# Router logits computed tile by tile inside the mix projection, first gather indices written by VectorE, gate splits behind the router

## The chip, the cores and the metric

One core of one Trainium2 chip runs the whole kernel in one launch. The metric is device time in microseconds (us). All times below are of that core.

## The reference

Two transformer-like blocks run one after the other on 1024 tokens of width 1024. The change touches the seam between attention and the mixture of experts in the first block. Cut to that:

```python
h = h + mix @ w_out[l]                      # mix projection, 1024 x 1024
xn = rmsnorm(h, ffn_norm_g[l])
g_prob = softmax(xt @ wg + bg)              # 4 groups
g_top_p, g_top_i = lax.top_k(g_prob, 1)
e_logits = (xt @ we + be)                   # 32 experts, the 8 of the chosen group
top_val, top_idx = lax.top_k(e_logits, 2)
# tokens are sorted into blocks of 128 per expert: buf_tok, block_e
xb = x_pad[buf_tok]                         # gather
h1 = silu(xblk @ w_gate[e]) * (xblk @ w_up[e]); y = h1 @ w_down[e]
```

The 4 group logits and 32 expert logits of a token are one product with a 1024 x 36 matrix. After the router, the tokens of each expert are gathered and go through its three weight matrices.

## The kernel before

The kernel is written engine by engine, each with its own program, and semaphores join them. Matrix products are made of fp16 halves: every fp32 operand is split into a high part (ScalarE, `..._hi`) and a low part (VectorE, `..._lo`), and `product` issues three matmuls (L409, L410, L411) for high by high, high by low and low by high.

**Mix projection.** Tokens are cut in 8 tiles of 128 (`TT`). For tile t TensorE runs two groups of 24 matmuls of 512 columns (`group`, banks of the PSUM tensor `ps`). VectorE adds the result to the residual (L1499), ScalarE takes the norm's statistics (L441, L442), VectorE scales to `xn` (L454). Two iterations later TensorE transposes `xn` of the tile (`transposes(pe, 2, t - 2, ...)`, 8 matmuls, L463) into the PSUM tensor `pt`, ScalarE copies the high part (`xt_hi`, L469), VectorE the low part (`xt_lo`, L475). `pt` has four banks. A transposed tile takes two of them, and `tpair(t % 2)` alternates between banks 0, 1 and banks 2, 3, so that the transposes of a tile wait for the low part of the tile but one before. Two tiles of transposes are left when the last group is done.

**Logits.** After all tiles TensorE computes the router logits: 8 tiles x 8 slices x 3 matmuls of 36 columns into bank 0 of `ps`, then one increment of `s_lg`.

**Router.** `router` on VectorE is a chain of some 60 small instructions, each waiting for the one before. It goes to TensorE three times and back. It ends with a table of which token stands in which place of which expert block: 16 matmuls (L1898) give the column numbers, VectorE turns them to integers (`tok_of`, L845) and increments `s_slots`. Just before that copy stand four small instructions for blocks beyond the first 32 (L838 to L843).

**Experts.** For block e, `gather` on GpSimd copies one column of `tok_of` to a fixed place (`idx[q]`, L997) and issues an indirect DMA by it (L1000). `x_transposes` on TensorE (L1908), `xe_hi` on ScalarE (L1178) and `xe_lo` on VectorE (L1518) make the halves of the gathered tokens in banks 0, 1 of `pt`. TensorE's order is transposes of block 0, transposes of block 1 (which wait for the low part of block 0), gate product of block 0, up product of block 0, gate product of block 1, and so on. The weights stand in slots: up in 0 and 1, gate in 2 and 3, down in 4 and one unsplit. `expert_hi` (L542) and `expert_lo` (L546) split them. VectorE splits the gate slots of expert 0 ahead of the router, the up slots behind it. SyncE loads the next expert's weights into a slot as soon as both halves of the present ones are made.

```python
            for i in range(2):
                expert_lo(dve, 2 + i, 0)
            router(dve, ch)
            for i in range(2):
                expert_lo(dve, i, 0)
            for q in range(2):
                xe_lo(q, q)
```

Of the kernel before, what the change touches and what calls it, by code (L numbers as in the profile page):

```python
# [15 lines left out]
P = 128  # L16
# [90 lines left out]
def build(nc, a, out):  # L107
    with ExitStack() as ctx:
# [52 lines left out]
        idx = [cols[:, 144 + i:145 + i].bitcast(I32) for i in range(2)]  # L161
        over_e = cols[0:1, 146:146 + NOVER + 1].bitcast(I32)
# [293 lines left out]

        def transposes(pe, r, t, src):
            n = TT * r + t
            pe.wait_ge(s_xn, n + 1)
            if n >= 2:  # L460
                pe.wait_ge(s_xl, n - 1)
            for k in range(KT):
                i = nc.tensor.transpose(tpair(t % 2)[:, k, :], src(t, k), ident)  # L463
            i.then_inc(s_tr, 1)

        def xt_hi(act, r, t):
            act.wait_ge(s_tr, TT * r + t + 1)
            dst = xh2(t) if r == 4 else XH[:, :, t * P:(t + 1) * P]
            nc.scalar.activation(dst, tpair(t % 2), ACT.Copy).then_inc(s_xh, 1)  # L469

        def xt_lo(dve, r, t):
            dve.wait_ge(s_xh, TT * r + t + 1)
            hi = xh2(t) if r == 4 else XH[:, :, t * P:(t + 1) * P]
            lo = xl2(t) if r == 4 else XL[:, :, t * P:(t + 1) * P]
            nc.vector.tensor_tensor(lo, tpair(t % 2), hi, ALU.subtract).then_inc(s_xl, 1)  # L475
# [85 lines left out]
        def overflow(eng, body):  # L561


            eng.wait_ge(s_slots, 1)
            n = eng.value_load(n_over, min_val=0, max_val=NOVER)
            with eng.If(n > 0):
                with eng.Fori(0, NOVER) as j:
                    with eng.If(j < n):
                        body(j)
# [178 lines left out]
        def router(dve, ch):  # L748
# [4 lines left out]
            dve.wait_ge(s_lg, 1)  # L753
            ch.done(V_.scalar_tensor_tensor(
                out=rL, in0=PS[:, 0, 0:TT * 36].rearrange("p (t c) -> p t c", t=TT), scalar=IWS,
# [80 lines left out]
            i.then_inc(s_rt, 1)  # L836

# [5 lines left out]
            V_.tensor_copy(n_over, rinc[0:1, NE - 1:NE])  # L843
            dve.wait_ge(s_rp, 3)
            V_.tensor_copy(tok_of, PS[:, 0, 0:BLK_MAX + 1]).then_inc(s_slots, 1)  # L845
# [107 lines left out]
        def _(pool):  # L953
# [41 lines left out]
            def gather(e, q):  # L995

                nc.gpsimd.tensor_copy(idx[q], tok_of[:, bass.ds(e, 1)]).then_inc(s_ix, 1)  # L997
                pool.wait_ge(s_ix, e + 1)
# [342 lines left out]
        def _(dve):  # L1341
# [166 lines left out]
            for i in range(2):  # L1508
                expert_lo(dve, 2 + i, 0)
            router(dve, ch)  # L1510


            for i in range(2):
                expert_lo(dve, i, 0)
# [217 lines left out]
        def _(pe):  # L1732
# [126 lines left out]
            for t in range(2):  # L1859
                transposes(pe, 1, t, mixed)  # L1860
            for t in range(TT + 2):
                if t < TT:
                    pe.wait_ge(s_xl, TT + t + 1)
                    for c in range(2):
                        g = 48 + 2 * t + c
                        group(pe, g, (12 + 2 * c, 13 + 2 * c), False, 0, t)
                        if g < 51:
                            for u in range(2):
                                transposes(pe, 1, 2 * (g - 47) + u, mixed)
                if t >= 2:  # L1870
                    transposes(pe, 2, t - 2, from_xn)

            pe.wait_ge(s_rws, 1)
            pe.wait_ge(s_xl, 3 * TT)
            for b in range(4):
                pe.wait_ge(s_free[b], 16)
            for t in range(TT):
                for k in range(KT):
                    tk, c = slice(t * P, (t + 1) * P), slice(k * 36, k * 36 + 36)
                    i = product(pe, PS[:, 0, t * 36:(t + 1) * 36], XH[:, k, tk], XL[:, k, tk], rwh[:, c], rwl[:, c],  # L1880
                                k == 0, k == KT - 1)
            i.then_inc(s_lg, 1)
# [284 lines left out]
```

## Time and profile before

| | us |
|---|---|
| median of 3 runs | 2337.84 |
| lowest, highest | 2336.97, 2340.63 |
| the profiled execution | 2341.51 |
| its span in the trace | 2339.8 |
| TensorE matmul busy | 2128.6 (91%) |
| VectorE busy | 1234.3 (53%) |
| ScalarE busy | 906.5 (39%) |

A row of the chain of waits gives start, length and what ran, followed back from the last instruction. A row of the timeline gives start, length, engine, line, operation, output and inputs, and in brackets how long the engine stood idle and what ended that. PE is TensorE, PEld its weight loads, DVE is VectorE, ACT ScalarE, POOL GpSimd, SPq the DMA queue of SyncE. Times are from the span's start.

### The profile page before, as it was taken

Reading aid. Unit: us, or ns where it says so; the run is one execution under the profiler, and the core shown is the slowest. Engines: PE = TensorE matmul, PEld = TensorE weight load, DVE = VectorE, ACT = ScalarE, POOL = GpSimd, SP = SyncE. Lnnn points to the kernel's source line nnn. Section 1 sums busy time; section 2 is a strip of 40 time slices with the busy share of each in tenths; the row PEclk is TensorE's granted clock in tenths of the full one; section 3 lists DMA queues with packets and bytes.
Section 4 is the critical chain, followed back from the end, with each engine's and each line's share of the span. In section 5 each row is a group of like instructions: output and inputs, shape, how many; then the busy total and the mean of one; then the engine's idle time right before and its main releaser. Section 6 shows DMA issues by size and latency. Waiting matters only on the chain.

```text
span 2339.8 us, 28085 instructions
## 1 busy us (share of the span) xinstructions
PE 2128.6 (91%) x10811; PEld 1091.7 (47%) x10811; DVE 1234.3 (53%) x1374; ACT 906.5 (39%) x1219; POOL 199.1 (9%) x264
## 2 busy tenths in 40 slices
PE   5998988888399999999945899959999999999999
PEld 3445446644244445445423465544444444444444
DVE  4225237744688888888867152384534343343432
ACT  4122126722267666666744152372312112211210
POOL 1000031000111111111120010022000000000000
PEclk9999999999699999999977899979999999999999
DMA  9101220051399999999975043325201011010001
GB/s 380 56 37 37 63 54 1 1 210 55 111 416 422 422 412 417 417 413 417 408 266 225 28 153 113 98 85 180 73 36 72 36 56 52 36 72 36 36 0 72
DMA packets 77020, 378.62 MB, mean 162 GB/s; under 512 B 12368, under 2 KB 19152, under 8 KB 44368
## 3 DMA queue, kind: packets, MB, share of 16 engines
q1 hardware_dynamic: 54000, 296.82, 32.1%
q0 software_dynamic: 22944, 80.75, 9.7%
q8 instruction: 52, 0.85, 0.2%
q14 instruction: 24, 0.20, 0.0%
HBM read 326.67 MB, written 37.75 MB: 156 GB/s over the span
## 4 chain that ended last, share of the span: by engine, by line
PE 86%; DVE 7%; issue 3%; DMA 2%; ACT 1%; SPq 1%; POOL 1%; POOLq 0%; DVEq 0%; ACTq 0%
PE ps L409 22%; PE ps L411 22%; PE ps L410 22%; PE pt L1954 5%; PE pt L409 1%; PE pt L410 1%; PE pt L411 1%; PE pt L1908 1%; DVE cols L1441 1%; PE pt L463 1%; PE pt L1844 1%; PE pt L2010 1%; PE pt L2012 1%; PE pt L2011 1%; DMA resid<-in_x 1%
## 5 line engine op out<-in xcount | busy, mean ns | idle before, releaser
L409 PE MATMUL ps<-xt,split 128*128 128x512 f16 x960 | 370.3, 386 | 22.8 <-issue 13.8
L409 PE MATMUL ps<-split,xt 128*128 128x512 f16 x928 | 354.5, 382 | 25.5 <-DMA xt<-arena 20.0
L410 PE MATMUL ps<-xt,split 128*128 128x512 f16 x960 | 369.7, 385 | 0.0
L411 PE MATMUL ps<-xt,split 128*128 128x512 f16 x960 | 369.4, 385 | 0.0
L411 PE MATMUL ps<-split,xt 128*128 128x512 f16 x928 | 354.4, 382 | 0.0
L410 PE MATMUL ps<-split,xt 128*128 128x512 f16 x928 | 354.3, 382 | 0.0
L546 DVE SCALAR_TENSOR_TENSOR split<-stage,split 128x2048 f16<-128x2048 f32 x128 | 290.1, 2287 | 57.8 <-ACT split L542 57.8
L542 ACT ACTIVATE split<-stage 128x2048 f16<-128x2048 f32 x128 | 237.1, 1901 | 121.1 <-PE ps L411 121.1
L411 PE MATMUL ps<-split,arena 128*128 128x512 f16 x512 | 194.3, 379 | 0.0
L410 PE MATMUL ps<-split,arena 128*128 128x512 f16 x512 | 194.3, 379 | 0.0
L409 PE MATMUL ps<-split,arena 128*128 128x512 f16 x512 | 194.3, 379 | 0.0
L1723 DVE SCALAR_TENSOR_TENSOR resid<-ps,resid 128x512 f32<-128x512 f32 x128 | 87.2, 690 | 191.7 <-PE ps L411 191.6
L409 PEld LDWEIGHTS ps<-xt,split 128*128 128x128 f16 x960 | 95.0, 99 | 139.0 <-issue 27.0
L1708 DVE TENSOR_TENSOR arena<-arena 128x512 f32<-128x512 f32 x64 | 44.3, 692 | 218.6 <-ACT arena L1322 218.6
L669 ACT ACTIVATE split<-stage 128x2048 f16<-128x2048 f32 x32 | 59.4, 1900 | 252.9 <-PE ps L411 252.9
L409 PEld LDWEIGHTS ps<-split,xt 128*128 128x128 f16 x928 | 91.3, 98 | 135.8 <-issue 35.2
L411 PEld LDWEIGHTS ps<-xt,split 128*128 128x128 f16 x960 | 95.2, 99 | 117.2 <-issue 6.9
L410 PEld LDWEIGHTS ps<-xt,split 128*128 128x128 f16 x960 | 95.1, 99 | 114.7 <-issue 5.5
L410 PEld LDWEIGHTS ps<-split,xt 128*128 128x128 f16 x928 | 91.2, 98 | 112.5 <-issue 12.5
L411 PEld LDWEIGHTS ps<-split,xt 128*128 128x128 f16 x928 | 91.2, 98 | 111.0 <-issue 2.7
L1322 ACT ACTIVATE arena<-ps 128x512 f32<-128x512 f32 x64 | 38.2, 597 | 244.1 <-PE ps L411 244.1
L1954 PE MATMUL pt<-arena,xt 128*128 128x512 f32 x256 | 115.1, 593 | 0.0
(291 smaller groups left out, 3010.3 us busy)
## 6 DMA issues: line engine op xcount, KB each, us to landing
stage<-in_w_gate SPq DMA_DIRECT2D x64, 1024.0 KB, 7.9
stage<-in_w_up SPq DMA_DIRECT2D x64, 1024.0 KB, 8.0
arena<-in_w_down SPq DMA_DIRECT2D x64, 1024.0 KB, 9.9
stage<-in_w_mlp SPq DMA_DIRECT2D x32, 1024.0 KB, 5.3
y_rows<-arena POOLq DMA_DIRECT2D x48, 512.0 KB, 8.7
arena<-in_conv_taps POOLq DMA_DIRECT2D x32, 576.0 KB, 4.3
stage<-in_w_dense_a SPq DMA_DIRECT2D x16, 1024.0 KB, 8.9
stage<-in_w_dense_b SPq DMA_DIRECT2D x12, 1024.0 KB, 9.0
```

What stands on the lines that cost most here:

```text
L409: nc.tensor.matmul(out_ap, lh, rh, start=start, stop=False)
L410: nc.tensor.matmul(out_ap, lh, rl, start=False, stop=False)
L411: return nc.tensor.matmul(out_ap, ll, rh, start=False, stop=stop)
L463: i = nc.tensor.transpose(tpair(t % 2)[:, k, :], src(t, k), ident)
L542: nc.scalar.activation(whi(s), wstage(s), ACT.Copy, scale=WS).then_inc(s_wh[s], 1)
L546: nc.vector.scalar_tensor_tensor(out=wlo(s), in0=wstage(s), scalar=WS, in1=whi(s), op0=ALU.mult, op1=ALU.subtract).then_inc(s_wo[s], 1)
L669: nc.scalar.activation(whi(s), wstage(s), ACT.Copy, scale=WS).then_inc(s_wh[s], 1)
L1322: nc.scalar.activation(relu[j % 2], PS[:, j % 4, :], ACT.Relu, scale=IWS)\
L1441: nc.vector.tensor_reduce(negmax[:, 2 * b + m:2 * b + m + 1], SC(m)[:, 0:W], AX.X, ALU.max, negate=True).then_inc(s_amx, 1)
L1708: nc.vector.tensor_tensor(relu2[j % 2], relu[j % 2], relu[j % 2], ALU.mult).then_inc(s_relu, 1)
L1723: nc.vector.scalar_tensor_tensor(out=H[:, t, hs], in0=PS[:, j % 4, :], scalar=IWS, in1=H[:, t, hs], op0=ALU.mult, op1=ALU.add).then_inc(s_ ...
L1954: m = nc.tensor.matmul(PT[:, 3, :], hTf[:, k, :], native(q)[:, k * UC:k * UC + UC], start=k == 0, stop=k == UK - 1)
```

## The change

Three things are done.

1. The logits of a tile are computed by a new function `logits(t)`, into bank 2 of `pt`. Tiles 0 to 4 come inside the mix projection, between the two groups of tiles 3 to 7. Tiles 5, 6 and 7 come between and behind the last transposes. Since bank 2 is taken, the transposes of this stage (r = 2) all use banks 0 and 1 (`tpar`), and each waits for the low part of the tile just before. Each of the eight `logits` increments `s_lg`, and the router waits for 8.
2. VectorE writes two columns of integer tokens straight to `idx[0]` and `idx[1]`, then `tok_of`, both ahead of the four small instructions. GpSimd's first two gathers have no copy of their own. The overflow code waits for a second increment of `s_slots`.
3. VectorE splits the gate slots behind the router: `router`, then slots 2, 3, 0, 1.

```diff
+        def tpar(r, t):
+            return tpair(0 if r == 2 else t % 2)
         def transposes(pe, r, t, src):
             n = TT * r + t
             pe.wait_ge(s_xn, n + 1)
-            if n >= 2:
+            if r == 2:
+                pe.wait_ge(s_xl, n)
+            elif n >= 2:
                 pe.wait_ge(s_xl, n - 1)
...
-            dve.wait_ge(s_lg, 1)
+            dve.wait_ge(s_lg, TT)
...
             i.then_inc(s_rt, 1)
+            dve.wait_ge(s_rp, 3)
+            V_.tensor_copy(idx2, PS[:, 0, 0:2])
+            V_.tensor_copy(tok_of, PS[:, 0, 0:BLK_MAX + 1]).then_inc(s_slots, 1)
...
-            V_.tensor_copy(n_over, rinc[0:1, NE - 1:NE])
-            dve.wait_ge(s_rp, 3)
-            V_.tensor_copy(tok_of, PS[:, 0, 0:BLK_MAX + 1]).then_inc(s_slots, 1)
+            V_.tensor_copy(n_over, rinc[0:1, NE - 1:NE]).then_inc(s_slots, 1)
...
             def gather(e, q):
-                nc.gpsimd.tensor_copy(idx[q], tok_of[:, bass.ds(e, 1)]).then_inc(s_ix, 1)
-                pool.wait_ge(s_ix, e + 1)
+                if not (isinstance(e, int) and e < 2):
+                    nc.gpsimd.tensor_copy(idx[q], tok_of[:, bass.ds(e, 1)]).then_inc(s_ix, 1)
+                    pool.wait_ge(s_ix, e - 1)
...
-            for i in range(2):
-                expert_lo(dve, 2 + i, 0)
             router(dve, ch)
-            for i in range(2):
-                expert_lo(dve, i, 0)
+            for s in (2, 3, 0, 1):
+                expert_lo(dve, s, 0)
...
+            def logits(t):
+                pe.wait_ge(s_rws, 1)
+                pe.wait_ge(s_xl, 2 * TT + t + 1)
+                for k in range(KT):
+                    tk, c = slice(t * P, (t + 1) * P), slice(k * 36, k * 36 + 36)
+                    i = product(pe, PT[:, 2, t * 36:(t + 1) * 36], XH[:, k, tk], XL[:, k, tk], rwh[:, c], rwl[:, c],
+                                k == 0, k == KT - 1)
+                i.then_inc(s_lg, 1)
             for t in range(TT + 2):
                 if t < TT:
                     pe.wait_ge(s_xl, TT + t + 1)
...
+                        if c == 0 and t >= 3:
+                            logits(t - 3)
                 if t >= 2:
                     transposes(pe, 2, t - 2, from_xn)
+                if t >= TT:
+                    logits(t - 3)
+            logits(TT - 1)
```

On TensorE, at the end of the mix projection, stood before: the last matmuls, three tiles of transposes (5, 6, 7), then 192 matmuls of 36 columns (line numbers of the changed kernel are one to some ten higher).

```order
2154 L411 MATMUL ps<-split,xt 128x512
2155 L463 MATMUL pt<-misc,xn 128x128 [waits xt_lo,norm_xn]
2156 L463 MATMUL pt<-misc,xn 128x128 x7
2157 L463 MATMUL pt<-misc,xn 128x128 [waits xt_lo,norm_xn]
2158 L463 MATMUL pt<-misc,xn 128x128 x7
2159 L463 MATMUL pt<-misc,xn 128x128 [waits xt_lo,norm_xn]
2160 L463 MATMUL pt<-misc,xn 128x128 x7
2161 L409 MATMUL ps<-zone,xt 128x36 [waits bank_free1,bank_free2,bank_free0,bank_free3,xt_lo,router_split]
```

And at the same place now:

```order
2274 L412 MATMUL ps<-split,xt 128x512
2275 L470 MATMUL pt<-misc,xn 128x128 [waits xt_lo,norm_xn]
2276 L470 MATMUL pt<-misc,xn 128x128 x7
2277 L470 MATMUL pt<-misc,xn 128x128 [waits xt_lo,norm_xn]
2278 L470 MATMUL pt<-misc,xn 128x128 x7
2279 L410 MATMUL pt<-zone,xt 128x36 [waits xt_lo,router_split]
...
2302 L412 MATMUL pt<-zone,xt 128x36
2303 L470 MATMUL pt<-misc,xn 128x128 [waits xt_lo,norm_xn]
2304 L470 MATMUL pt<-misc,xn 128x128 x7
2305 L410 MATMUL pt<-zone,xt 128x36 [waits xt_lo,router_split]
```

24 of the small matmuls stand between the transposes of tiles 6 and 7, 48 behind them, and the other 120 have moved ahead of this place, 24 at a time.

On VectorE, from the end of the router to the first gathered block, stood before (`router_products` is `s_rp`, `w_hi` the high half of a weight slot, `x_hi` the high half of a gathered block):

```order
406 L834 TENSOR_TENSOR junk<-junk,misc 128x384
407 L838 TENSOR_TENSOR arena<-arena,misc 1x512
408 L841 TENSOR_REDUCE arena<-arena 1x16 [waits dve_step]
409 L842 TENSOR_SCALAR cols<-arena 1x16 [waits dve_step]
410 L843 CAST cols<-arena 1x1
411 L845 CAST cols<-ps 128x48 [waits router_products]
412 L546 SCALAR_TENSOR_TENSOR split<-stage,split 128x2048 [waits w_hi0]
413 L546 SCALAR_TENSOR_TENSOR split<-stage,split 128x2048 [waits w_hi1]
414 L1518 TENSOR_TENSOR xt<-pt,xt 128x1024 [waits x_hi] x2
```

And now:

```order
404 L841 TENSOR_TENSOR junk<-junk,misc 128x384
405 L845 CAST cols<-ps 128x2 [waits router_products]
406 L846 CAST cols<-ps 128x48
407 L848 TENSOR_TENSOR arena<-arena,misc 1x512
408 L851 TENSOR_REDUCE arena<-arena 1x16 [waits dve_step]
409 L852 TENSOR_SCALAR cols<-arena 1x16 [waits dve_step]
410 L853 CAST cols<-arena 1x1
411 L553 SCALAR_TENSOR_TENSOR split<-stage,split 128x2048 [waits w_hi2]
412 L553 SCALAR_TENSOR_TENSOR split<-stage,split 128x2048 [waits w_hi3]
413 L553 SCALAR_TENSOR_TENSOR split<-stage,split 128x2048 [waits w_hi0]
414 L553 SCALAR_TENSOR_TENSOR split<-stage,split 128x2048 [waits w_hi1]
415 L1523 TENSOR_TENSOR xt<-pt,xt 128x1024 [waits x_hi] x2
```

The integer copies moved ahead of the four small instructions, and four splits stand where two stood.

On GpSimd, behind the eight stores of `xn`, stood before:

```order
27 L997 COPY cols<-cols 128x1 [waits slots_known,norm_transposed,xn_stored1,xn_stored0]
28 L1000 DMA xt<-xn_rows,cols 128x1024 [waits index_column]
29 L997 COPY cols<-cols 128x1
30 L1000 DMA xt<-xn_rows,cols 128x1024 [waits index_column]
31 L997 COPY cols<-cols 128x1 [waits x_gathered0,x_transposed]
```

And now:

```order
27 L1009 DMA xt<-xn_rows,cols 128x1024 [waits norm_transposed,slots_known,xn_stored0,xn_stored1]
28 L1009 DMA xt<-xn_rows,cols 128x1024
29 L1006 COPY cols<-cols 128x1 [waits x_gathered0,x_transposed]
```

The two copies ahead of the first two indirect DMAs are gone.

## Rows read from the trace of the kernel before

**Rows 1.** The page, part 4: shares of the chain that ended last

```profile
PE 86%; DVE 7%; issue 3%; DMA 2%; ACT 1%; SPq 1%; POOL 1%; POOLq 0%; DVEq 0%; ACTq 0%
```

**Rows 2.** Chain of waits, 500 to 660 us: start, length, what ran

```profile
613.40 3.87 POOL cols L997
...
618.15 6.47 DMA xt<-xn_rows,cols
624.76 1.95 PE pt L1908 x8
...
627.79 1.24 DVE xt L1518
629.16 1.94 PE pt L1908 x8
631.11 0.43 PE ps L409
```

**Rows 3.** Timeline, VectorE, 570 to 665 us

```profile
577.54 1.23 DVE L475 TENSOR_TENSOR xt<-pt,xt 128x1024 f16<-128x1024 f32 x1 [1.06 <-ACT xt L469]
...
582.39 1.23 DVE L475 TENSOR_TENSOR xt<-pt,xt 128x1024 f16<-128x1024 f32 x1 [1.11 <-ACT xt L469]
584.19 4.49 DVE L546 SCALAR_TENSOR_TENSOR split<-stage,split 128x2048 f16<-128x2048 f32 x2 [0.57 <-ACT split L542]
589.46 0.46 DVE L754 SCALAR_TENSOR_TENSOR arena<-ps,zone 128x288 f32<-128x288 f32 x1 [0.78 <-PE ps L411]
...
611.06 0.67 DVE L838 TENSOR_TENSOR arena<-arena,misc 1x512 f32<-1x512 f32 x1
...
612.63 0.18 DVE L845 CAST cols<-ps 128x48 int32<-128x48 f32 x1
612.74 4.47 DVE L546 SCALAR_TENSOR_TENSOR split<-stage,split 128x2048 f16<-128x2048 f32 x2
```

**Rows 4.** Timeline, TensorE, 574 to 613 us

```profile
574.19 1.04 PE L463 MATMUL pt<-misc,xn 128*128 128x128 f32 x8
576.53 1.09 PE L463 MATMUL pt<-misc,xn 128*128 128x128 f32 x8 [1.30 <-DVE xn L454]
...
588.34 0.18 PE L411 MATMUL ps<-zone,xt 128*128 128x36 f16 x1
...
588.94 0.18 PE L411 MATMUL ps<-zone,xt 128*128 128x36 f16 x1
...
611.20 0.82 PE L1898 MATMUL ps<-junk,arena 128*128 128x48 f16 x16 [9.94 <-DVE junk L834]
```

**Rows 5.** Windows: stretch, length, busy time by engine, then clock, DMA share, GB/s

```profile
570.00:574.00 4.00, 4.00 (x21) 1.78 (x19) 0.00 (x0) 0.00 (x0) 0.00 (x0) 1.00 0.00 0
...
581.00:582.00 1.00, 0.30 (x3) 0.06 (x1) 0.29 (x1) 0.66 (x1) 0.00 (x0) 0.71 0.46 188
...
588.00:589.00 1.00, 1.00 (x45) 1.00 (x42) 0.69 (x1) 0.00 (x0) 0.00 (x0) 0.87 0.71 262
...
700.00:800.00 100.00, 100.00 (x451) 49.56 (x450) 85.03 (x58) 68.34 (x58) 16.11 (x18) 1.00 1.01 422
```

**Rows 6.** Timeline, ScalarE, 570 to 665 us

```profile
577.66 1.02 ACT L469 ACTIVATE xt<-pt 128x1024 f16<-128x1024 f32 x1 [0.16 <-PE pt L463]
```

**Rows 7.** Timeline, GpSimd and VectorE, where experts end and combining begins

```profile
1206.09 2.78 POOL L1045 DMA_INDIRECT arena<-y_rows,cols  x1 [4.13 <-issue]
...
1215.08 0.94 POOL L1045 DMA_INDIRECT arena<-y_rows,cols  x1 [0.30 <-issue]
...
1201.31 8.90 DVE L595 SCALAR_TENSOR_TENSOR split<-stage,split 128x2048 f16<-128x2048 f32 x4 [0.44 <-issue]
1215.07 2.61 DVE L1573 SCALAR_TENSOR_TENSOR resid<-arena,cols,resid 128x1024 f32<-128x1024 f32 x2 [4.86 <-DMA arena<-y_rows,cols]
```

**Rows 8.** Timeline, SyncE's DMA queue, 570 to 665 us

```profile
586.56 2.55 SPq L536 DMA_DIRECT2D stage<-in_w_gate  x2
615.10 2.93 SPq L536 DMA_DIRECT2D stage<-in_w_up  x2
```

More of the change, by code:

```diff
@@ L161, in build @@
         idx = [cols[:, 144 + i:145 + i].bitcast(I32) for i in range(2)]
+        idx2 = cols[:, 144:146].bitcast(I32)
         over_e = cols[0:1, 146:146 + NOVER + 1].bitcast(I32)
@@ L459, in transposes @@
             pe.wait_ge(s_xn, n + 1)
-            if n >= 2:
+            if r == 2:
+                pe.wait_ge(s_xl, n)
+            elif n >= 2:
                 pe.wait_ge(s_xl, n - 1)
             for k in range(KT):
-                i = nc.tensor.transpose(tpair(t % 2)[:, k, :], src(t, k), ident)
+                i = nc.tensor.transpose(tpar(r, t)[:, k, :], src(t, k), ident)
             i.then_inc(s_tr, 1)
@@ L468, in xt_hi @@
             dst = xh2(t) if r == 4 else XH[:, :, t * P:(t + 1) * P]
-            nc.scalar.activation(dst, tpair(t % 2), ACT.Copy).then_inc(s_xh, 1)
+            nc.scalar.activation(dst, tpar(r, t), ACT.Copy).then_inc(s_xh, 1)
         def xt_lo(dve, r, t):
@@ L474, in xt_lo @@
             lo = xl2(t) if r == 4 else XL[:, :, t * P:(t + 1) * P]
-            nc.vector.tensor_tensor(lo, tpair(t % 2), hi, ALU.subtract).then_inc(s_xl, 1)
+            nc.vector.tensor_tensor(lo, tpar(r, t), hi, ALU.subtract).then_inc(s_xl, 1)
         FM = [True, False, False, True, True, False]
@@ L561, in overflow @@
         def overflow(eng, body):
-            eng.wait_ge(s_slots, 1)
+            eng.wait_ge(s_slots, 2)
             n = eng.value_load(n_over, min_val=0, max_val=NOVER)
@@ L752, in router @@
             tok = misc[:, M_TOK:M_TOK + TT]
-            dve.wait_ge(s_lg, 1)
+            dve.wait_ge(s_lg, TT)
             ch.done(V_.scalar_tensor_tensor(
-                out=rL, in0=PS[:, 0, 0:TT * 36].rearrange("p (t c) -> p t c", t=TT), scalar=IWS,
+                out=rL, in0=PT[:, 2, 0:TT * 36].rearrange("p (t c) -> p t c", t=TT), scalar=IWS,
                 in1=rb.unsqueeze(1).to_broadcast([P, TT, 36]), op0=ALU.mult, op1=ALU.add))
@@ L1869, in _ @@
                                 transposes(pe, 1, 2 * (g - 47) + u, mixed)
+                        if c == 0 and t >= 3:
+                            logits(t - 3)
                 if t >= 2:
                     transposes(pe, 2, t - 2, from_xn)
-            pe.wait_ge(s_rws, 1)
-            pe.wait_ge(s_xl, 3 * TT)
+                if t >= TT:
+                    logits(t - 3)
+            logits(TT - 1)
             for b in range(4):
                 pe.wait_ge(s_free[b], 16)
[L1877 to L1882, printed above, removed]
             pe.wait_ge(s_rt, 1)
```

## Prediction

> **What bounds the kernel now.** I read the shares of the chain first: TensorE holds 86% of it [rows 1], so time is won where TensorE stands still or does work that could be elsewhere. The chain in order of time then shows the one long stretch where it does: from the last groups of the mix projection to the gate product of expert 0. TensorE waits there in turn for the router, for a 3.87 us copy on GpSimd, for a 6.47 us indirect DMA, and for the round through ScalarE and VectorE, until 631.11 [rows 2]. Behind it, in the expert loop, TensorE is busy in 100.00 of 100 us, and ahead of it, in the mix projection, in 4.00 of 4 us [rows 5]. So all that counts is the moment at which the gate product starts. What makes it earlier is won in full, and what is added to the mix projection is lost in full.
>
> I count from two moments: S = 574.19, when the transposes of tile 5 start [rows 4], and R = 589.46, when the router's first instruction starts [rows 3]. R is S + 15.27.
>
> **Logits inside the projection: +3.0.** The logits at the end ran mostly at the lower clock; the clock rose to 2.4 GHz at the end of the 588 to 589 window (granted 0.87 on average), and from there the rows stand 0.025 us apart: 24 of them take 588.94 - 588.34 = 0.60 us [rows 4, 5]. Inside the projection the clock is high, so a tile costs 0.60 us, and five tiles (0 to 4) cost 3.0 us on an engine that has no slack. Nothing hides this. The bounds are 2.0 (if 36 columns cost by their number) and 4.0 (if each switch between 512 and 36 columns costs 0.2 more). Their operands are ready: the low part of the tile is a whole group old. S moves by +3.0.
>
> **The tail: -2.0.** Before, the transposes of tile 6 started at 576.53, beside the low part of tile 5, since they used other banks. Now they wait for it: it ends at 577.54 + 1.23 = 578.77, which is S + 4.6 [rows 3, 4]. From a tile's transposes to ScalarE's copy pass 577.66 - 576.53 = 1.13, the copy takes 1.02 [rows 6], and the low part 1.23: 3.4 us with the hand-over. So tile 6 is done at S + 8.0, and only then may tile 7 be transposed. At full clock it is done at S + 11.5. Before, the clock fell in the 581 to 582 window (0.71), 6 us after the dense work of the projection ended, though two tiles of transposes lay between [rows 5]. Now tile 7's transposes come 7 us after it. I take them at 1.2 GHz: 1.95 for eight instead of 1.09 [rows 2, 4], so S + 12.3. The logits of tiles 5 and 6 lie beside the waits. Those of tile 7 take 24 x 0.03 and a drain of 0.2, 0.9 us, so the router starts at S + 13.2 instead of S + 15.27: -2.0 (at full clock -3.0). The 7 x 0.7 us of logits that go from here are so half eaten by the single pair of banks. With the +3.0 before S, the router starts 1.0 us later than now.
>
> **Gate splits behind the router.** Ahead of the router they cost nothing: 584.19 to 588.68, beside the logits [rows 3]. With logits short they would now hold the router up, so moving them is what makes the shorter tail worth anything. Behind the router there is no cover but the gather.
>
> **From router to gate product: -5.0.** The router itself does not change. Its last matmuls end at 611.20 + 0.82 = 612.02 [rows 4]. VectorE now copies at once: 612.1 to 612.35 with 0.18 each, overlapping as consecutive ones do; before, the copy ended at 612.81, behind the four small instructions. These follow, from 611.06 to 612.74 before, less the copy: 1.6 us, so the splits start at 613.9. Four take 8.90 [rows 7]: 622.8. Then comes the low part of block 0 with 1.24, to 624.0; the transposes of block 1 0.14 later, as before (629.16 after 627.79 + 1.24), with 1.95: the gate product starts at 626.1 against 631.11, if the gather is ready [rows 2, 3].
>
> The gather: 0.6 us passed from the copy's end to GpSimd's (612.81 to 613.40) and 0.9 from that one's end to the DMA (617.27 to 618.15) [rows 2, 3]. One wait is left, so the DMA starts between 613.0 and 613.9, lands 6.47 later, by 619.5 to 620.4, and the low part may start 627.79 - 624.76 = 3.03 after that, at 622.5 to 623.4. VectorE is free at 622.8. The two ways to the low part are level: I add 0.2. So the 4.8 us that the GpSimd copy and its hop give back are real, but VectorE's two added splits stand right behind them. Any further speed of the gather would be worth nothing.
>
> **Loads.** A slot is reloaded when both its halves are made. The gate loads of expert 1 went out at 586.56, the up loads at 615.10 [rows 8]. They now go out from 616 to 623, four of 1 MB, beside the gathers. At the loop's 422 GB/s [rows 5] 4 MB and the two gathers take 12 us, so all is there by about 629; ScalarE first needs them when the gate product is over, some 6 us after 626.1. Free, if the gathers are not held up by them; if they are, by up to 1.4 us.
>
> **Sum.** +3.0 - 2.0 - 5.0 + 0.2 = -3.8 us. The profiled execution took 2341.51, 1.7 more than its span and 3.7 more than the median; the terms are differences, so 2341.51 becomes 2337.7 and the median 2337.84 becomes 2334.0.
>
> **Rival 1, full clock in the tail (2333.1).** If the clock has not yet fallen at S + 8, the last round is 0.85 shorter and the last logits 0.1: -4.75. For it: the drop came only 6 us after the dense work. Against: by then there have been two long waits of TensorE.
>
> **Rival 2, the port (2339.1, or 2343.3 at worst): slower.** The GpSimd copy that took 3.87 ended at 617.27, and the two splits beside it at 612.74 + 4.47 = 617.21 [rows 2, 3]. It seems to have waited for them. If an indirect DMA is held off by splits in the same way, it now meets four of them. The second gather is issued near 614.7, within the splits in any case. Held to 622.8 it lands at 629.3, and the gate product starts at 631.2, 5.1 later than summed: 2334.0 + 5.1 = 2339.1. The first gather is issued at 613.0 to 613.9, the splits start at 613.9; if it misses that moment too, it lands at 629.3, the low part starts at 632.3, the gate product at 635.6: +9.5 - 0.2, so 2343.3, slower than before. For it: an indirect DMA issued at 1206.09 inside four splits took 2.78 instead of 0.94. Against: it ended at 1208.87, 1.3 before those splits did (1210.21), so it got in between two of them; and one beside another two-input VectorE instruction (1215.07) took the usual 0.94 [rows 7]. Let in after the first split, the second gather lands by 622.6, soon enough.
>
> The Trainium skill, "SBUF — State Buffer", section "Who interferes with whom", speaks for the strong form: a VectorE instruction with two inputs in SBUF contends with a GpSimd instruction that reads SBUF, and the pair is held for the whole instruction. By that rule the trace agrees for the copy (3.87 beside two splits) and disagrees for the DMA of 1215.08 (0.94).
>
> **Rival 3, crowded gathers or dearer logits (2335.5).** Gathers beside the weight loads land 1.4 later, or each switch to 36 columns costs 0.2 to 0.3 more: +1.0 to +1.5.
>
> **Rival 4, nothing won at the back.** If the 3.87 us were a cost of GpSimd's first instruction after a long rest, not of the copy, the indirect DMA would bear it: it would start near 617.3, the low part near 626.8, 4.0 late, and the sum is near zero: 2338. Against: the copy's end fits the splits' end within 0.1.
>
> **Chances.** The forecast 0.46, rival 1 0.22, rival 2 0.13 (0.08 at 2339.1, 0.05 at 2343.3), rival 3 0.13, rival 4 0.06. The range 2331.5 to 2339.5 takes in all but the worst form of rival 2 and the scatter of runs. A measurement of this kernel can tell about 0.2%, 4.7 us, from no change. Under 2333.2 fall rival 1 in half its cases and some of the forecast's scatter, 0.28; above 2342.5 the worst of rival 2, 0.07; between them 0.65.
>
> **What would show it.** Right: rows of 36 columns 0.025 us apart inside the projection, 0.60 per tile; the last low part of the norm about 1 us later than 582.39; the router's start near 590.4; the first indirect DMA some 0.7 to 1.5 us after the copy, with no GpSimd row ahead; xe_lo of block 0 starting straight behind the fourth split; the gate product near 627.3. Wrong: transposes of tile 7 in 1.09 (rival 1); an indirect DMA longer than 2 us, or the second set of block transposes waiting for DMA (rival 2, 3); a first indirect DMA of 4 us (rival 4); a different rate in the expert loop.

## The result and the profile after

The changed kernel takes 2344.7 us (median of 8 runs, 2342.79 to 2347.66). The kernel before, run beside it, takes 2337.4 (8 runs, 2335.77 to 2340.63). The ratio is 1.0033 [1.0023, 1.0042]: slower by 7.3 us, where 3.8 us of gain were forecast. The whole measured interval lies above the predicted range.

The profiled execution took 2347.66 with a span of 2345.9, against 2341.51 and 2339.8: +6.1 in the span. The chain of the changed kernel, in order of time (start, length, what ran), answers to [rows 2]:

```profile
577.35 0.70 DVE resid L1508
...
580.50 1.24 DVE xt L482
581.87 1.96 PE pt L470 x8
583.85 1.03 ACT xt L476
584.90 1.24 DVE xt L482
586.28 1.96 PE pt L470 x8
588.25 1.03 ACT xt L476
589.31 1.24 DVE xt L482
591.60 0.47 DVE arena L761
...
615.87 1.03 POOL xt L1009
616.89 0.30 issue
617.20 16.37 DMA xt<-xn_rows,cols
633.57 0.04 issue
633.61 1.97 PE pt L1919 x8
635.58 0.43 PE ps L410
```

The GpSimd copy of 3.87 is gone from the chain, and a DMA of 16.37 us stands where one of 6.47 stood. It is the second gather, not the first. The timelines of GpSimd and VectorE, changed kernel, show why:

```profile
615.87 1.03 POOL L1009 DMA_INDIRECT xt<-xn_rows,cols  x1 [31.93 <-issue]
617.20 8.58 POOL L1009 DMA_INDIRECT xt<-xn_rows,cols  x1 [0.30 <-issue]
...
614.33 0.20 DVE L846 CAST cols<-ps 128x48 int32<-128x48 f32 x1
...
615.99 0.13 DVE L853 CAST cols<-arena 1x1 int32<-1x1 f32 x1
616.05 8.88 DVE L553 SCALAR_TENSOR_TENSOR split<-stage,split 128x2048 f16<-128x2048 f32 x4
624.86 1.20 DVE L1523 TENSOR_TENSOR xt<-pt,xt 128x1024 f16<-128x1024 f32 x1
```

The first gather is issued at 615.87 and is in time: the low part of block 0 follows straight behind the fourth split, at 624.86. The second is issued at 617.20, 1.15 us after the four splits began, and GpSimd is busy with it until 625.78. The splits end at 624.93. Its data arrive only at 633.57.

I measure positions from three marks, because the moment at which the projection ends differs between profiles of kernels whose front parts are the same: by up to 2.4 us with the front part of before (574.39 before, 571.96 and 572.10 in two of the kernels below), by up to 3.7 with that of the changed kernel (574.66 to 578.31 in nine kernels). **E** is the start of the last evacuation of the projection (the `resid` row at 577.35), **R** the start of the router (591.60), **G** the first 512-column matmul of the gate product, as the chain gives it (635.58).

| kernel | E | E to R | R to G | what VectorE does behind the router |
|---|---|---|---|---|
| before | 574.39 | 15.07 | 41.65 | two splits, beside a GpSimd copy |
| changed | 577.35 | 14.25 | 43.98 | four splits, second gather held |

E to R is 0.82 better, R to G 2.33 worse, and E itself is 2.96 later. Together G is 4.47 later. The 2.96 alone prove little, given how E scatters; the means are 576.2 for the nine kernels with the logits in the projection and 573.0 for the five others, 3.2 apart.

### The profile page after: what moved, and what is told of

The parts are those of the page before. It is cut to its first block, busy times and chain, and to the rows that moved or that the text cites. A ratio compares the mean times of both kernels' runs of the same rounds, so it can differ in the third digit from the quotient of the medians.

```text
span 2345.9 us, 28062 instructions
## 1 busy us (share of the span) xinstructions
PE 2131.8 (91%) x10811; PEld 1091.8 (47%) x10811; DVE 1233.7 (53%) x1375; ACT 906.7 (39%) x1219; POOL 205.0 (9%) x262
## 4 chain that ended last, share of the span: by engine, by line
PE 84%; DVE 6%; SPq 3%; DMA 3%; issue 2%; ACT 1%; POOL 0%; POOLq 0%; DVEq 0%; ACTq 0%
PE ps L410 22%; PE ps L411 22%; PE ps L412 22%; PE pt L1965 5%; SPq L644 2%; PE pt L410 1%; PE pt L412 1%; PE pt L411 1%; PE pt L470 1%; DVE cols L1450 1%; PE pt L1919 1%; PE pt L1849 1%; PE pt L2023 1%; PE pt L2022 1%; PE pt L2021 1%
## 5 line engine op out<-in xcount | busy, mean ns | idle before, releaser
L470 PE MATMUL pt<-misc,xn 128*128 128x128 f32 x288 | 47.6, 321 | 75.2 <-DVE xn L1593 40.8
```

Of the source, the lines that this page charges most:

```text
L470: i = nc.tensor.transpose(tpar(r, t)[:, k, :], src(t, k), ident)
```

## The experiments

All twelve kernels compute the whole reference.

**1. Holding the splits back (a1_wait).** VectorE waits, behind the router, for a count that GpSimd raises behind the second gather:

```diff
+            pool.sem_inc(s_gi, 1)          # behind gather(1, 1)
...
             router(dve, ch)
+            dve.wait_ge(s_gi, 1)
             for s in (2, 3, 0, 1):
```

> The changed kernel, with one wait added: VectorE starts the four splits behind the router only when GpSimd has issued both first gathers. Theory (the splits hold up the second indirect DMA): it takes about 1 us instead of 8.58, the splits run from about 618.4 to 627.3, the gate product of expert 0 starts near 630.5 instead of 635.6, total about 5 us under the changed kernel, near 2339.5. Rival (the second indirect DMA is slow by itself): it keeps its 8.6 us, VectorE waits for it, the gate product starts near 638 and the total is near 2347.

Measured: 0.9997 [0.9987, 1.0007] against before. GpSimd, VectorE and the chain of a1_wait:

```profile
614.46 2.17 POOL L1010 DMA_INDIRECT xt<-xn_rows,cols  x1 [0.30 <-issue]
...
613.25 0.13 DVE L854 CAST cols<-arena 1x1 int32<-1x1 f32 x1
613.49 8.90 DVE L554 SCALAR_TENSOR_TENSOR split<-stage,split 128x2048 f16<-128x2048 f32 x4
...
614.46 9.36 DMA xt<-xn_rows,cols
```

The edit did not do what it was meant to. The splits start 0.97 us ahead of the second gather's issue, so the count rose before that issue ran. But two things are different by a little: the gather comes 0.97 into the first split, where it was 1.15, and the splits begin 0.11 behind the end of VectorE's last small copy, where they had begun 0.07 ahead of it. One of them, or both, sufficed: the gather is through at 616.63, 0.91 behind the end of the first split (613.49 + 2.23 = 615.72), instead of at the end of all four. R to G falls from 43.98 to 36.96. The low part of block 0 is issued at the same distance from the splits' start as before (8.81), so behind the router the two kernels differ in the second gather only. Those 7.0 us are the price of its being held. Even so the gather is not early: it lands at 623.82, 0.2 after VectorE's side is ready, and later than the 622.6 of the prediction.

**2. The gathers' columns alone (a2_gather).** The logits and the splits stand as in the kernel before; only the two integer copies on VectorE, in place of GpSimd's, are kept.

> The kernel before, with only the integer columns written by VectorE and the first two gathers without their copy (logits and gate splits as before). Theory: the first indirect DMA starts near 613.7 instead of 618.15; the second, issued near 615, is held until the two up splits end near 618.3; the gate product starts between 626.6 and 629 instead of 631.1; total 2 to 4.5 us under the kernel before, 2333 to 2335.5. Rival (the gain of the copy is lost in the gathers in any order): total within 1 us of the kernel before.

Measured: 1.0002 [0.9991, 1.0014]. GpSimd, VectorE and the chain of a2_gather:

```profile
613.37 4.18 POOL L1003 DMA_INDIRECT xt<-xn_rows,cols  x1 [0.30 <-issue]
...
612.23 4.47 DVE L547 SCALAR_TENSOR_TENSOR split<-stage,split 128x2048 f16<-128x2048 f32 x2
...
613.37 12.22 DMA xt<-xn_rows,cols
```

With two splits the second gather is held as well, until 0.85 us after they end (616.70 to 617.55). R to G is 39.75, 1.9 better than before and 4.7 worse than d5 below, which has the same two splits behind a gather that is out. The hold thus scales with the row of splits: 4.18 beside 4.47, 8.58 beside 8.88. The 2 to 4.5 us that the theory expected in the total did not come: 1.9 us lie within the interval, and in this profile E to R is 15.89, 0.8 longer than before.

**3. The loads out of the gathers' way (a3_loads).** The loads for expert 1 wait until block 1 has landed:

```diff
+                if first and q == 0:
+                    sp.wait_ge(s_gx[1], 16)
                 if not (last and q):
                     expert_load(sp, "gate", e + 1)
```

> The changed kernel, with SyncE holding back the next weight loads (gate and up of expert 1) until the second gather has landed. Theory (the hold ends near 625.8, and the landing then took 7.8 us more because four 1 MB loads were under way): the indirect DMA still takes 8.6 us, but lands near 629.7 instead of 633.6; the gate product starts near 631.7, about 3.9 us under the changed kernel, near 2341. Rival (only the hold counts): the gather lands near 633.6 as in the changed kernel, total the same or later.

Measured: 1.0008 [0.9999, 1.0018]. The chain of a3_loads:

```profile
618.14 11.76 DMA xt<-xn_rows,cols
...
630.37 10.80 DMA stage<-in_w_gate
```

The gather is held as in the changed kernel (618.14, 8.58, 1.14 into the splits), but its data are there 3.2 us after GpSimd is through (626.72 to 629.90) instead of 7.8 (625.78 to 633.57). So the four weight loads beside it cost 4.6 us of its landing. R to G is 39.37. But ScalarE then waits for the gate weights until 641.16, and from G to the down block of the last expert pass 570.5 us instead of 567.8: 2.7 of the 4.6 are gone again in this profile. Of these, 1.1 are not the loads' doing: the last expert's twelve matmuls run longer at the lower clock here (5.10 instead of 4.01, see the last section). The profiled execution was the slowest of ten (2344.95, median 2339.24), and by the ratios a3_loads is 0.25% under the changed kernel, some 6 us, so the runs do not show that much is lost again. The loads make the hold dearer; without the hold the landing ends TensorE's wait by 0.2 us in run 1, and by 1.0 in run 6, where it comes 8.3 us after the end of the issue (624.85, with VectorE's low part of block 0 done at 623.8).

**4. The logits alone (b1_logits).** Logits inside the projection and on one pair of banks; the copies and the splits as before.

> Only the first part of the change: logits tile by tile with the single pair of banks; gate splits ahead of the router and the copies on GpSimd as before. Theory: the mix projection ends 3.0 us later, the last low part is done near 590.5, the gate splits wait for ScalarE (589.2 to 592.9) and end near 595.6, the router starts there instead of at 589.5, everything behind it as before: the gate product near 637.3, total 6.2 us over the kernel before, near 2343.6. Rival (the tail is not slower, only the gathers are): total within 1 us of the kernel before.

Measured: 1.0026 [1.0017, 1.0036]. E to R is 18.16, 3.9 longer than in the changed kernel: the pair of gate splits, 4.49, stands between the last low part and the router, and no logits are left that would hide them. R to G is 41.83, as before. This bears out that the splits had to move if the logits did, and that part one is a loss by itself.

**5. Later splits (d3_later).** The changed kernel with two copies of one column ahead of the splits, some 0.4 us:

```diff
+            for _ in range(2):
+                ch.done(nc.vector.tensor_copy(cols[:, 163:164], cols[:, 164:165]))
             for s in (2, 3, 0, 1):
```

> The changed kernel with two tiny chained copies ahead of the four splits, so that these start some 0.4 us later and the second indirect DMA is issued about 0.75 us into the first split instead of 1.15. Theory (it depends on the moment whether GpSimd gets in between two splits): it gets in at the first boundary, as with the added wait (2.2 us), and the gate product starts some 37 us behind the router's start. Rival (four splits in a row hold it whenever it is issued within them): 8 us or more, 44 us.

**6. Gaps between the splits (d2_gap).** The changed kernel in which each split waits for the one before it to have ended:

```diff
+            for j, s in enumerate((2, 3, 0, 1)):
+                if j:
+                    dve.wait_ge(s_wo[(2, 3, 0, 1)[j - 1]], BASE[0] + 1)
```

> The changed kernel, each split waiting until the one before has ended, which opens a gap of about 0.1 us between them. Theory (back-to-back splits leave GpSimd no opening): the second indirect DMA, issued 1.15 us into the first split, ends about 1 us behind that split: some 2 us instead of 8.58. Rival (it must wait until VectorE has no split left): 8 us or more.

Measured, one run each: 2337.81 and 2338.73, beside 2336.84 for before. GpSimd and VectorE of d3_later, then of d2_gap:

```profile
617.19 2.35 POOL L1009 DMA_INDIRECT xt<-xn_rows,cols  x1 [0.30 <-issue]
...
616.39 8.90 DVE L553 SCALAR_TENSOR_TENSOR split<-stage,split 128x2048 f16<-128x2048 f32 x4
```

```profile
614.53 1.97 POOL L1009 DMA_INDIRECT xt<-xn_rows,cols  x1 [0.30 <-issue]
...
613.38 9.24 DVE L553 SCALAR_TENSOR_TENSOR split<-stage,split 128x2048 f16<-128x2048 f32 x4
```

Both set the gather free at the first boundary. In d3_later the gather is issued 0.80 into the first split; the two copies also leave VectorE 0.03 us of rest ahead of the splits (616.36 to 616.39), where the changed kernel has none. In d2_gap it is issued 1.15 into it, exactly as in the changed kernel, and the only difference is that a split starts some 0.1 us later after the one before it, so that no two overlap: the hold goes from 8.58 to 1.97. So neither the number of splits nor their sum holds the gather: it takes splits that stand back to back. That alone does not hold it either, as a1_wait and d3_later show, whose splits do so too. R to G is 36.96 and 37.96.

**7. Splits behind a gather that is really out (d4_issued, d5_cols_issued).** A memset of one column on GpSimd stands behind the second gather and raises the count that VectorE waits for. d4 is the changed kernel with it, d5 the kernel before with VectorE's copies and it (its gate splits stay ahead of the router, so that only the two up splits are held back):

```diff
+            nc.gpsimd.memset(cols[:, 163:164], 0.0).then_inc(s_gi, 1)   # behind gather(1, 1)
...
             router(dve, ch)
+            dve.wait_ge(s_gi, 1)
```

> The changed kernel with the four splits held back until a tiny GpSimd instruction behind the second gather has run. Theory: second indirect DMA 1 us; the splits start some 26.8 us behind the router's start and the gate product 39 (43.98 in the changed kernel); total some 5 us under the changed kernel and within 2.5 us of the kernel before, since the router still starts later there. Rival (only the lost time in the gather was wrong in the forecast): 3 us or more under the kernel before.

> The kernel before with the integer columns only, and with VectorE's two up splits held back until a tiny GpSimd instruction behind the second gather has run. Logits and gate splits as before. Theory: second indirect DMA 1 us, gate product 36 to 37.5 us behind the router's start (41.65 before, 39.75 with the columns alone): total 4 to 5 us under the kernel before. Rival (landing, not issue, decides): the second gather still lands late beside the up loads, total within 2.5 us of the kernel before.

Measured: d4 1.0008 [0.9999, 1.0018], d5 0.9981 [0.9971, 0.9992]. GpSimd and VectorE of d4:

```profile
615.41 0.97 POOL L1010 DMA_INDIRECT xt<-xn_rows,cols  x1 [0.30 <-issue]
616.38 0.12 POOL L1022 MEMSET cols<- 128x1 f32 x1
...
616.53 8.90 DVE L554 SCALAR_TENSOR_TENSOR split<-stage,split 128x2048 f16<-128x2048 f32 x4 [2.19 <-POOL cols L1022]
```

With no split beside it the second gather takes 0.97. In d4 VectorE loses 2.19 us of waiting and has four splits after it, so R to G is 38.83. In d5 R to G is 35.04, 6.6 less than before and 1 better than expected; in the total 4.4 us of it show. It is the best of the runs with the second part of the change alone, and it beats the kernel before.

**8. The changed kernel without VectorE's copies (b2_nocols).**

> The changed kernel without the integer columns (the copies on GpSimd are back): parts 1 and 3 of the change. Theory (the copy is held as long as splits follow one another without a gap): the copy takes 8.3 to 8.5 us instead of 3.87, the gate product starts some 46 us behind the router's start, total 6 to 8 us over the kernel before. Rival (the copy gets in behind the first or second split): 4 us or less, 41 us.

Measured, one run: 2348.39 beside 2336.69. GpSimd and VectorE:

```profile
613.39 8.26 POOL L1004 COPY cols<-cols 128x1 int32<-128x1 int32 x1 [31.68 <-DVE cols L852]
...
612.73 8.88 DVE L553 SCALAR_TENSOR_TENSOR split<-stage,split 128x2048 f16<-128x2048 f32 x4
```

One element per partition is copied in 8.26 us. Beside two splits it was 3.87 [rows 2, 3]. The copy ends when the splits do (621.65 and 621.61), so it too waits for the whole row, and both gathers come after it: R to G is 47.43. The total is 11.7 over, not the 6 to 8 expected. Logits +3.0, tail -0.8 and R to G +5.8 make 8.0; a lower clock in the last expert adds 1.4 in this profile, and the rest of this one run is not traced. Rival 4 falls with it: the copy's length follows VectorE's row and is no fixed cost of GpSimd's first instruction.

**9. A later second gather (e1_offset).** The changed kernel with eight further counts (`pool.sem_inc(s_seen, 1)`) on GpSimd's queue between the gathers, to shift the moment of issue.

> The changed kernel with eight idle counts on GpSimd between the two gathers, so that the second is issued later within the first split than the 1.15 us of the changed kernel. Theory A (whoever asks later than about 1.1 us into a split has missed the opening at its end, and those behind it): held to the end of the last split, 7 us or more. Theory B (only the moment about 1.15 us is unlucky): it gets in at the end of the first or second split, under 3.5 us.

Measured, one run: 2346.17 beside 2336.69. GpSimd of e1_offset:

```profile
615.39 8.58 POOL L1009 DMA_INDIRECT xt<-xn_rows,cols  x1 [0.30 <-issue]
```

The gap between the gathers is 0.30 as ever, and the splits start at 614.25, so the moment is 1.14 again. The shift did not happen: the eight counts are through between 613.84 and 614.41, while the first gather is still being issued (614.07 to 615.09). The run only repeats the hold. It doesn't tell whether the moment is what decides.

**10. What the logits could have done (d1_tail, e2_order).** Both keep the two pairs of transpose banks and put the logits into TensorE's gaps in the tail, not into the projection: they go to bank 0 of `ps`, free once its last group is read. The copies are VectorE's, and the splits wait for the memset of 7. d1 makes three splits ahead of block 0's low part and one behind it; e2 makes two ahead, one between the two low parts and one behind:

```diff
                 if t >= 2:
                     transposes(pe, 2, t - 2, from_xn)
+                if t >= TT - 1:
+                    for u in {TT - 1: (0, 1), TT: (2, 3, 4), TT + 1: (5, 6)}[t]:
+                        logits(u)
...
+            dve.wait_ge(s_gi, 1)           # e2
+            for s in (2, 3):
+                expert_lo(dve, s, 0)
+            xe_lo(0, 0)
+            expert_lo(dve, 0, 0)
+            xe_lo(1, 1)
+            expert_lo(dve, 1, 0)
```

> A kernel of my own: logits stay in bank 0 of ps, so that the two pairs of transpose banks stay, and are computed tile by tile in the gaps of the last three transposes only, none inside the mix projection; integer columns as in the change; all four splits of expert 0 behind the router, and behind a tiny GpSimd instruction that follows the second gather, in the order gate, gate, up, low part of block 0, up. Theory: the router starts 4.5 to 5 us earlier relative to the end of the projection (10.5 instead of 15.1 behind the last bank read), the second indirect DMA takes 1 us, the gate product starts 36 to 37.5 us behind the router's start instead of 41.65: together about 9 us under the kernel before, near 2329. Rival (time won ahead of the expert loop is lost again in it, because the weight loads start later): the gate product starts early, but the total is under by less than 4 us.

> The kernel with the logits in the gaps of the tail, one thing changed: behind the gathers VectorE makes gate, gate, low part of block 0, up, low part of block 1, up, so that only two splits stand ahead of the low part of block 0. Theory (VectorE's third split was the last thing late there): the gate product starts some 35 us behind the router's start instead of 36.7, the total is about 1.5 us lower than with that kernel, 9 to 10 under the kernel before. Rival (the up splits, now later, hold the up product up): the same total.

Measured: d1 0.9965 [0.9952, 0.9978], e2 0.9961 [0.9947, 0.9975] (2324.83 to 2331.09 in five runs): both beat both kernels, e2 by 9.1 us against before, d1 by 8.2. The two intervals overlap, so whether e2's order is worth anything in the total is not shown. TensorE of d1_tail, then a window of d1_tail (stretch, length, busy time of PE, PEld, DVE, ACT, POOL, then clock, DMA share, GB/s):

```profile
578.72 1.09 PE L465 MATMUL pt<-misc,xn 128*128 128x128 f32 x8 [0.79 <-DVE xn L456]
```

```profile
581.00:582.00 1.00, 0.00 (x1) 0.00 (x0) 1.00 (x1) 1.00 (x1) 0.00 (x0) 1.00 0.35 139
```

E to R is 10.17 and 10.16, against 15.07 before and 14.25 in the changed kernel. The logits fill the gaps, the last transposes run in 1.09 as before (1.96 in the changed kernel), and the clock is 1.00 in the window in which it had fallen to 0.71 before; it falls at 584.1, 11 us after E, when the router has begun. R to G is 36.66 in d1 and 35.19 in e2.

## Why the prediction was wrong

**Logits inside the projection: +3.0, right.** The rows of 36 columns start 0.025 us apart (559.54, 559.57, 559.59, 559.62). The evacuations of VectorE, changed kernel and then before, show the price of a tile:

```profile
565.52 0.69 DVE L1508 SCALAR_TENSOR_TENSOR resid<-ps,resid 128x512 f32<-128x512 f32 x1 [5.02 <-PE ps L412]
571.64 0.69 DVE L1508 SCALAR_TENSOR_TENSOR resid<-ps,resid 128x512 f32<-128x512 f32 x1 [1.75 <-PE ps L412]
577.35 0.69 DVE L1508 SCALAR_TENSOR_TENSOR resid<-ps,resid 128x512 f32<-128x512 f32 x1 [5.02 <-PE ps L412]
```

```profile
563.16 0.69 DVE L1499 SCALAR_TENSOR_TENSOR resid<-ps,resid 128x512 f32<-128x512 f32 x1 [4.42 <-PE ps L411]
569.28 0.69 DVE L1499 SCALAR_TENSOR_TENSOR resid<-ps,resid 128x512 f32<-128x512 f32 x1 [1.75 <-PE ps L411]
574.39 0.69 DVE L1499 SCALAR_TENSOR_TENSOR resid<-ps,resid 128x512 f32<-128x512 f32 x1 [4.42 <-PE ps L411]
```

One half of a tile takes 6.12 in both (569.28 - 563.16, 571.64 - 565.52), the half with the logits 5.71 instead of 5.11: +0.60, five times.

**The tail: -2.0, it was -0.8.** (Three tiles of transposes are left when the last group is done, 5, 6 and 7; the description of the kernel before says two.) Counted from the transposes of tile 5 (577.15 now), tile 5 is done after 4.59, as summed (4.6). The step that fails is the next, "So tile 6 is done at S + 8.0": it takes tile 6's transposes at full clock, 1.09. They took 1.96, and tile 6 was done after 8.99. The windows of the changed kernel:

```profile
580.00:581.00 1.00, 0.00 (x0) 0.00 (x0) 0.50 (x1) 0.47 (x1) 0.26 (x1) 1.00 0.17 70
581.00:582.00 1.00, 0.13 (x1) 0.16 (x2) 0.96 (x3) 0.00 (x0) 0.00 (x0) 0.54 1.02 418
```

TensorE had done nothing from 578.2 to 581.87, and the clock had fallen when it began tile 6. Before, the fall also came in the 581 to 582 window, but there this was some 7 us after E and tiles 6 and 7 had been transposed by then; now it is some 4 us after E. I had taken the time to the fall (6 us in the prediction's count, from the end of the dense work) [rows 5] for a property of the clock, though TensorE had worked in between, and had weighed only that the clock might hold longer (rival 1). It was not even fixed for the tail of before: a2_gather has that tail, and there the clock fell in the 576 to 577 window, 4.2 us after E, so that tile 7's transposes took 1.97. With the changed tail tile 6's transposes took 1.94 to 1.96 in eight of nine kernels. That is 0.85 of the 1.2; two hand-overs of 0.13 that I took as included and the last logits make up the rest. In a1_wait tile 6 took 1.55 and E to R 13.84. The forecast's list of signs also held a slip: the last low part "about 1 us later than 582.39" contradicts its own sum, which puts it at 588.3; it started at 589.31.

**Splits behind the router: right.** b1_logits shows what they cost ahead of it.

**Router to gate product: forecast 36.8, and 36.96 where the second gather gets in (a1_wait, d3_later).** VectorE's own side was exact: the copies at R + 22.66 (forecast 22.64), the splits at R + 24.45 (24.44), and the transposes of block 1 at R + 34.99 in a1_wait (34.9 with the 0.2). The step that failed is the sentence "Let in after the first split, the second gather lands by 622.6, soon enough", on which the sum rested. Rival 2's first form came true, the second gather held to the end and the first in time. I gave it 0.08, on the strength of one row, the issue at 1206.09 that got in [rows 7] (which begins its row of splits after 0.44 us of rest, unlike this one), and wrote off the copy of 3.87 that had waited for two splits as another kind of instruction. It was the same kind of wait.

Its price was too small as well. For this case R to G was put at 41.7 (631.2 less 589.46); it measured 43.98. Of the difference 0.85 is GpSimd's own time after the last split, which I had left out (the issue ends at R + 34.18, where R + 33.3 was put), and 1.3 is the landing: 6.5 us after the end of the issue in the forecast, 7.8 in the trace, in a stretch where the DMA engines moved 415 GB/s. The 1.4 that rival 3 put on crowding was about right in size, but it fell on a gather that was already late.

The Trainium skill, "SBUF — State Buffer", section "Who interferes with whom", says that a VectorE instruction with two SBUF inputs and a GpSimd instruction that reads SBUF exclude each other for the whole instruction. The trace agrees that the gather's issue is excluded by these splits, and disagrees on the length: 8.58 us is not one split of 2.2 but all that was left of four. By the rule of one instruction the gather would have been let in at the end of the first split, after some 2 us, as in d2_gap (1.97), which comes at the same moment.

**Behind the gate product's start: forecast at nothing, +1.6 in this profile.** The windows of the changed kernel show the lower clock in the product's first 3.5 us (635.58 to 639.1):

```profile
638.00:639.00 1.00, 1.00 (x4) 0.39 (x3) 1.00 (x1) 0.00 (x0) 0.00 (x0) 0.50 0.71 176
639.00:640.00 1.00, 1.00 (x5) 0.39 (x4) 1.00 (x1) 0.00 (x0) 0.00 (x0) 0.94 0.91 332
```

Before, it rose about 1.5 us after 631.11. At half speed the additional 2.0 us cost 1.0. TensorE had stood for 11.30 us for the second block here, but that this is why is not shown: in d3_later it stood for 4.31 and the clock rose 3.7 us after G, in a3_loads 6.72 and 1.3. The other part is in the last expert. TensorE of the changed kernel, then of before, on the same twelve matmuls:

```profile
1199.41 0.61 PE L410 MATMUL pt<-arena 128*128 128x512 f16 x1 [1.97 <-DVE arena L1545]
...
1203.42 1.02 PE L1965 MATMUL pt<-arena,xt 128*128 128x512 f32 x2
```

```profile
1193.93 0.39 PE L409 MATMUL pt<-arena 128*128 128x512 f16 x1 [1.97 <-DVE arena L1540]
...
1196.54 1.02 PE L1954 MATMUL pt<-arena,xt 128*128 128x512 f32 x2
```

They take 4.01 instead of 2.61, +1.4, behind the same idle 1.97 us. So G to this point is 567.8 against 565.4. This +1.4 is in part the luck of two profiles: seven of all fourteen have it, with and without the held gather (last section). What follows is 0.8 shorter in the profile of after; I did not trace that, and over all profiles this rest differs by up to 4 us.

**The account.** In the profiles: E +3.0, tail -0.8, router to gate product +2.3, lower clock in two places +2.4, the end -0.8: +6.1, the difference of the spans. The forecast was +3.0, -2.0, -4.8 and 0.0, which is -3.8. The miss of 9.9 is 1.2 in the tail, 7.1 by the held gather and what stands beside it, and 1.6 behind. The medians differ by 7.3, the two spans by 6.1; this 1.2 is less than single executions of one kernel differ by, and I did not look for it. Without the last expert and the end, which the change does not touch, 5.5 us are explained; the interval of the runs is 5.4 to 9.8, so up to 4 us more may be open.

**Range and chances.** The upper end of 2339.5 took in the held gather at 2339.1, but with a price too small by 2, and not together with a smaller gain in the tail, though the two are independent. The time fell in the part beyond 2342.5 that I gave 0.07.

## What to carry to other kernels

- Where VectorE runs a row of instructions back to back on two SBUF operands, expect that a GpSimd copy or indirect DMA that falls into it may be held until the end of the row, and look at who waits for it. Either issue it first and make VectorE wait for a real GpSimd instruction behind it (0.12 us), or leave gaps in the row.
- Removing a slow instruction (the copy of 3.87) does not remove what made it slow. The next instruction on that queue inherits it: ask what stood beside it.
- Small matmuls cost their full time in a stage that TensorE bounds, and nothing in the gaps of a latency-bound one; there they also keep the clock up for what follows.

## What was not expected of the hardware

**Whether GpSimd gets in: the moment, or how the row begins.** An indirect DMA reaching the row 1.14 or 1.15 us after its start was held to the end (the changed kernel, a2, a3, e1: four of four with splits back to back). At 0.80 (d3) and 0.97 (a1), and in the combine stage at 0.37 into the third split (1206.09, 2.78 long [rows 7]), it got in at the next boundary. The copy was held at 0.66 (before, b1, b2). With 0.1 us more from split to split, 1.15 got in too (d2).

The moment alone is no rule. The copies at 0.66 were held, gathers at 0.80 and 0.97 were not, and GpSimd's later copies in a1, d1, d3 and d4 came 1.5 to 1.9 us into a split with another one right behind it and got in at the next boundary (in d4 at 620.59, 0.47 long). In the fourteen profiles there are 28 cases in which a copy or an indirect DMA met a split with a further one right behind it. Another mark than the moment separates them all: the seven that were held fell into rows whose first split began on the heels of VectorE's small copy (615.99 + 0.13 against 616.05; the same in [rows 3]), and the 21 that got in fell into rows that began after some rest of VectorE (0.03 us in d3, 0.11 in a1, 0.44 in the combine stage, 2.2 in d1 and d4). No run changes one of the two marks and leaves the other, since the one meant for it, e1, did not move; which of them counts, and why, is open. Plain DMAs that GpSimd issues were not held at all: the one at 1201.42 of before took 0.53 inside the first of four splits.

**GpSimd's count behind an indirect DMA comes early.** In a1_wait the splits that wait for it began 0.97 us before the DMA's own issue; eight counts between two gathers in e1_offset were through before the first gather's issue had ended and delayed nothing. A memset of 0.11 to 0.12 us behind the gather does order it.

**A gather's landing depends on its company.** From the end of its issue to its landing, 512 KB took 3.2 us with no weight load beside it (a3_loads), 5.5 beside two (before, the first gather, 619.17 to 624.62), 7.2 in a1_wait, 7.8 in the changed kernel, 7.0 in d3_later and 8.3 in d2_gap, beside four. It is not the number alone: in a2_gather, with two loads, the second gather took 8.0. The windows of the changed kernel and of a3_loads over the landing:

```profile
626.00:633.50 7.50, 0.00 (x0) 0.00 (x0) 0.06 (x1) 0.00 (x0) 0.97 (x1) 0.50 1.00 415
```

```profile
626.70:629.90 3.20, 0.00 (x0) 0.00 (x0) 0.31 (x1) 0.00 (x0) 1.18 (x3) 0.50 0.64 189
```

In the first the DMA engines have no free share (1.00), in the second 0.64 is used.

**The last expert has two speeds.** Behind the same 1.97 us of rest, the twelve matmuls begin at the lower clock in seven of thirteen profiles besides that of before (the changed kernel, a2, a3, b2, d2, d3, e1) and at full clock in the others (a1, b1, d1, d4, d5, e2). 1.4 us of a kernel's time hang on that, and no single part of the change goes with it. What does go with it is the gate product of the first expert: in six of the seven the clock had risen 2.9 to 3.9 us after G there, in the seven others, before included, 1.0 to 2.5 us after. The seventh, a3_loads, had 1.3, but its loop had waited for the weights. Whether the one leads to the other was not tested; what sets it stays open.
